# Second block's attention: value products of two pairs of heads' units in one go, six buffers for turned probabilities, the other heads' units placed by fours

## What is computed

```
heads = concat(o_a, o_b, o_c)
h = layer_norm(DEEPNORM_ALPHA * x + heads @ w_o, ln1_g, ln1_b)
ffn = (silu(h @ w_gate) * (h @ w_up)) @ w_down
return layer_norm(DEEPNORM_ALPHA * h + ffn, ln2_g, ln2_b)
```

## Time and profile before

| what | us |
|---|---|
| median of 3 runs | 1861.59 |
| the profiled execution | 1860.51 |
| its span in the trace | 1858.7 |
| TensorE busy in the span | 1830.9 |
| the attention loop, first layer of the second block | about 747 to 826 in the trace |
| the same, second layer | about 1360 to 1439 |

### The profile page before, as it was taken

One profiled execution on the slowest core, in us unless ns is written; L12 is line 12 of the kernel. 1 busy time (PEld: TensorE's weight loads), 2 busy tenths in 40 slices (PEclk: granted clock), 3 DMA queues, 4 the chain that ended last, 5 costly groups with the idle time before them and its releaser, 6 DMA issues.

```text
span 1858.7 us, 26490 instructions
## 1 busy us (share of the span) xinstructions
PE 1830.9 (99%) x10358; PEld 1532.0 (82%) x10358; DVE 771.7 (42%) x1679; ACT 802.7 (43%) x1571; POOL 790.6 (43%) x639
## 2 busy tenths in 40 slices
PE   8999999999999999999999999999999999999997
PEld 6888887888887888768888888888876898888886
DVE  4575575376473454876111110065377621111003
ACT  5222386472376565872323222127488233222213
POOL 2433372265553453334444444435322444444442
PEclk9999999999999999999999999999999999999999
DMA  9554412124402243103333333223310333333321
GB/s 331 195 151 152 131 46 69 57 91 141 138 24 71 71 139 95 58 25 91 91 110 95 91 94 133 87 87 108 118 47 19 94 102 100 91 91 113 114 91 45
DMA packets 195242, 185.60 MB, mean 100 GB/s; under 512 B 24150, under 2 KB 162564, under 8 KB 195120
## 3 DMA queue, kind: packets, MB, share of 16 engines
q1 hardware_dynamic: 180520, 172.51, 29.4%
q10 hardware_dynamic: 14600, 11.41, 2.2%
HBM read 179.11 MB, written 5.44 MB: 99 GB/s over the span
## 4 chain that ended last, share of the span: by engine, by line
PE 89%; ACT 4%; POOL 2%; DVE 2%; issue 1%; SPq 1%; DMA 1%; DVEq 0%; ACTq 0%; POOLq 0%
PE ps L1536 25%; PE ps L1538 25%; PE ps L1537 25%; PE ps L2079 3%; PE ps L2196 2%; PE ps L2175 2%; POOL w_lo L833 1%; PE ps L1598 1%; PE ps L1615 1%; PE ps L1631 1%; PE ps L2171 1%; ACT pt L1026 1%; ACT w_hi L968 1%; ACT sc L1016 1%; PE ps L1557 1%
## 5 line engine op out<-in xcount | busy, mean ns | idle before, releaser
L833 POOL TENSOR_TENSOR w_lo<-raw,w_hi 128x512 fp32r<-128x512 f32 (+1 forms) x505 | 671.0, 1360 | 828.3 <-ACT w_hi L968 828.1
L968 ACT ACTIVATE w_hi<-raw 128x1024 fp32r<-128x1024 f32 (+1 forms) x273 | 255.2, 980 | 262.6 <-PE ps L1538 190.9
L1536 PE MATMUL ps<-g_hi,w_lo 128*128 128x512 f32 (+1 forms) x928 | 348.4, 375 | 0.7 <-POOL w_lo L833 0.7
L1537 PE MATMUL ps<-g_lo,w_hi 128*128 128x512 f32 (+1 forms) x928 | 347.4, 374 | 0.0
L1538 PE MATMUL ps<-g_hi,w_hi 128*128 128x512 f32 (+1 forms) x928 | 347.4, 374 | 0.0
L1536 PEld LDWEIGHTS ps<-g_hi,w_lo 128*128 128x128 f32 x928 | 174.7, 188 | 33.0 <-POOL w_lo L833 1.1
L1537 PEld LDWEIGHTS ps<-g_lo,w_hi 128*128 128x128 f32 x928 | 174.7, 188 | 31.1
L1538 PEld LDWEIGHTS ps<-g_hi,w_hi 128*128 128x128 f32 x928 | 174.7, 188 | 31.0
L2940 DVE TENSOR_TENSOR tmp_f<-ps,tmp_f 128x512 f32<-128x512 f32 x44 | 30.4, 692 | 370.0 <-PE ps L1538 370.0
L1536 PE MATMUL ps<-h_hi,w_lo 128*128 128x512 f32 (+1 forms) x496 | 176.9, 357 | 0.1
L1537 PE MATMUL ps<-h_lo,w_hi 128*128 128x512 f32 (+1 forms) x496 | 174.6, 352 | 0.0
(11 more groups left out here) (305 smaller groups left out, 3229.6 us busy)
## 6 DMA issues: line engine op xcount, KB each, us to landing
raw<-in_w_in SPq DMA_DIRECT2D x33, 1024.0 KB, 5.1
raw<-in_w_mod SPq DMA_DIRECT2D x24, 1024.0 KB, 6.6
raw<-in_w_gate SPq DMA_DIRECT2D x44, 512.0 KB, 3.8
raw<-in_w_up SPq DMA_DIRECT2D x44, 512.0 KB, 4.9
raw<-in_w_down SPq DMA_DIRECT2D x22, 1024.0 KB, 4.8
raw<-in_w_out SPq DMA_DIRECT2D x8, 1024.0 KB, 5.0
strips<-bias_rows ACTq DMA_DIRECT2D x18, 256.0 KB, 4.1
raw<-in_w_o SPq DMA_DIRECT2D x4, 1024.0 KB, 4.9
```

Of the source, the lines that this page charges most:

```text
L833: pool.tensor_tensor(w_lo[:, i % SPLIT, a:e], raw_of(what)[:, a:e], w_hi[:, i % SPLIT, a:e].bitcast(F32), ALU.subtract).then_inc(s_tile_lo ...
L968: act.activation(w_hi[:, i % SPLIT, a:b], raw_of(what)[:, a:b], ACT.Copy).then_inc(s_tile_hi.sem, s_tile_hi.nth((what, n)))
L1536: pe.matmul(o, lhs[1], rhs[0], start=first, stop=False)
L1537: pe.matmul(o, lhs[0], rhs[1], start=False, stop=False)
```

## The change

`N_P` goes from 4 to 6. The two new buffers lie in parts of `qa` that nothing uses. `upto` becomes 4, 8, 12, 12, 16, 20, 24, 24, 28, 32, 36, 36, so the a and c units come in fours (two pairs), and after two of the 12 b pairs none come; 12 are left for the end. `DEFERRED` holds the ranks of 12 pairs a layer, the first pair of each four. Their value product is not made at its own place but directly ahead of that of the second pair, into columns 128 to 255 of the second pair's bank, and VectorE moves both out one after the other. The bank of a deferred rank is free as soon as ScalarE has copied the turned probabilities.

```diff
+        pt2 += [at(f"pt2_{4 + i}", [P, SEQ], names["qa"][0] + 4 * SEQ * (2 * i + 1)) for i in range(2)]
...
-                upto = 2 * ((n + 1) * 17 // len(pairs[EARLY // 2:]))
+                upto = 4 * -(-(n + 1) * 9 // len(pairs[EARLY // 2:]))
...
-        N_S, N_T, N_B, N_P = 3, 5, 5, 4
+        N_S, N_T, N_B, N_P = 3, 5, 5, 6
...
+        DEFERRED = set()
+        for r, i in enumerate(RANKS[:-2]):
+            if UNITS[i]["half"] == UNITS[RANKS[r + 2]]["half"] == 1 and r - 2 not in DEFERRED:
+                DEFERRED.add(r)
...
-                    if u["half"] == 0:
+                    if u["half"] == 0 or r in DEFERRED:
                         return
...
+                    for second, o in ((r - 2, P), (r, 0)) if r - 2 in DEFERRED else ((r, 0),):
+                        n = len(UNITS[RANKS[second]]["vs"])
+                        for j in range(n):
+                            for half in range(2):
+                                one = second - 1 + half
+                                m = pe.matmul(ps[HD * half:HD * half + HD, b, o:o + P], UNITS[RANKS[one]]["vs"][j],
+                                              pt2[one % N_P][:, P * j:P * j + P], start=j == 0, stop=j == n - 1)
+                        m.then_inc(s_mixed.sem, s_mixed.nth((y, second)))
...
-                        emptied[b] = s_pt.after((y, r)) if UNITS[i]["half"] == 0 else s_o_out.after((y, r))
+                        emptied[b] = s_pt.after((y, r)) if UNITS[i]["half"] == 0 or r in DEFERRED else s_o_out.after((y, r))
...
-                        V.tensor_copy(into, ps[:, b, 0:P]).then_inc(s_o_out.sem, s_o_out.nth((y, r)))
+                        for second, o in ((r - 2, P), (r, 0)) if r - 2 in DEFERRED else ((r, 0),):
+                            x = UNITS[RANKS[second]]
+                            into = ao_t[:, AO_T[CHUNK_OF[x["kind"], x["head"]]], P * x["i"]:P * x["i"] + P]
+                            V.tensor_copy(into, ps[:, b, o:o + P]).then_inc(s_o_out.sem, s_o_out.nth((y, second)))
```

More of the change, by code:

```diff
@@ L680, in _program @@
         LAST = len(RANKS) - 1
+        DEFERRED = set()
+        for r, i in enumerate(RANKS[:-2]):
+            if UNITS[i]["half"] == UNITS[RANKS[r + 2]]["half"] == 1 and r - 2 not in DEFERRED:
+                DEFERRED.add(r)
+        assert len(DEFERRED) == (A_HEADS + C_HEADS) // 2 * XT // 2 and not any(
+            r in DEFERRED and RANKS[r + 2] != RANKS[r] + 2 for r in range(len(RANKS)))
         MIXED_WITH = [r + 1 if UNITS[i]["half"] == 0 else r for r, i in enumerate(RANKS)]
@@ L2167, in mix @@
                         pe.wait_ge(s_proj.sem, s_proj.at((y, "vc", XT - 1)))
-                    n = len(u["vs"])
-                    for j in range(n):
-                        if u["half"] is None:
+                    if u["half"] is None:
+                        n = len(u["vs"])
+                        for j in range(n):
                             m = pe.matmul(ps[:, b, 0:HD], pt2[r % N_P][:, P * j:P * j + P], u["vs"][j], start=j == 0, stop=j == n - 1)
[L2172 to L2177, removed]
+                        m.then_inc(s_mixed.sem, s_mixed.nth((y, r)))
+                        return
+                    for second, o in ((r - 2, P), (r, 0)) if r - 2 in DEFERRED else ((r, 0),):
+                        n = len(UNITS[RANKS[second]]["vs"])
+                        for j in range(n):
+                            for half in range(2):
[3 more added lines that the diff above has]
+                        m.then_inc(s_mixed.sem, s_mixed.nth((y, second)))
                 for i in range(EARLY + 2, EARLY + N_S):
```

## The result

| | before | changed |
|---|---|---|
| median, us | 1861.37 (1860.95 to 1862.58, 4 runs) | 1880.70 (1879.21 to 1881.98, 4 runs) |
| profiled execution, us | 1860.51 | 1881.98 |
| its span in the trace | 1858.7 | 1880.2 |
| mean granted clock | 0.998 | 0.994 |
| loop of the first layer | 80.46 | 91.10 |

The changed kernel is slower: ratio 1.0102, interval 1.0087 to 1.0117, 19.3 us between the medians. The prediction was 1866.0, range 1856 to 1871.5, so the time lies outside it. A loop is counted here from the start of its first transposes to the start of the last record of its last value product; the row of that product has 4 records before and 12 in the changed kernel. The two loops together are 20.2 us longer, of 21.5 us in the spans: the change acted where it was made, and almost nowhere else.

What follows compares the result with a forecast made beforehand. TensorE was taken to set the pace. Per layer, savings of 3.25 and old waits of 1.6 gone against 7.4 of new waits gave +2.5, +5.1 in both: 1865.6, put at 1866.0 us, range 1856 to 1871.5.

Steps and rivals of the forecast that it cites:

- What bounds the kernel: Whole kernel and both attention loops: TensorE sets the pace, busy 77.3 of 78.9 us in the loop stretch, clock 1.00.
- What TensorE saves: Attention loops: 12 fewer visits and 21 fewer changes of arrangement a layer save 3.25 us a layer, 6.5 in both.
- Rival 4: Joint value products: two pairs in one go pay the surcharge again, only the new waits are left; 1872 us, chance 0.04.
- the drain of 0.053 us: TensorE's changes of tiling mode: about 128 cycles each at full clock, by which 42 fewer would save 2.2 us.
- units 29, 49, 55 and 61: TensorE's transposes waiting for VectorE's joinings: 3.0 us at units 27 to 29, then 2.0, 0.9 and 0.55 a layer.
- The lead sum: Unit 29: TensorE's 3.56 us between unit 28's scores and 29's transposes against VectorE's 5.1; at least 1.5 us of waiting.
- ScalarE's lateness: Steps 24 to 27: ScalarE has 5.1 us against TensorE's 3.95, so unit 27's exponential comes about 1.5 us late.
- No DMA and no GpSimd work moves: Whole change: DMA and GpSimd work stay where they were, counted at nothing.
- The parts at nothing: New buffers, copies out in twos, DMA, GpSimd and the rest of the kernel: no net cost, within 0.2 us for the rest.
- Units 67 to 72 and the end of the loop: Late in each loop: 0.6 us waiting for unit 73's score bank, and 0.35 at the end from copies and norm steps.
- gone from the old order: Old order's waits that vanish: 0.65 at the b3 pair, some 0.35 at 767.70, a few smaller; about 1.6 us a layer.
- Rival 1: Joinings: VectorE runs ahead, waits don't grow, only saved visits count; 1854.0, up to 1857.5 us, chance 0.18.

Runs made afterwards that it cites:

- the even order: Changed kernel with four other units behind each of the first nine b pairs, no two b pairs side by side, 11 pairs deferred: 1868.55 us, ratio 1.0042.

## Why the prediction was wrong

The direction was right, slower. The size was not: 4.6 us were forecast over the kernel before, 19.3 were measured.

**What bounds the kernel: right, but one quantity was taken as fixed.** TensorE sets the pace in the loops, and time was lost by making it wait and by what came behind the waits. The clock of 1.00 in the earlier trace rows was read as a property of the stretch. It held in a loop whose longest wait was some 0.8 us; behind waits of 1.3 to 2.3 us it was 0.50 for 17.0 us. Here is the step that failed: the sum prices a wait at its own length, at a clock of 1.00 throughout. What the clock costs behind a wait is absent from the sum and from every rival, and it is the largest single error: 7.6 us by the rows in those stretches (4.3 and 3.3), 9.5 by the comparison with filled waits. The span's mean clock says the same: 0.998 to 0.994 of 1880 us is 7.5.

The Trainium skill's page "TensorE: Matmul & The Clock Gate", Part 1, says that throttled is the default state of TensorE's clock and that activity releases it, and puts the cost of the ramp below 1% of a typical span. The trace agrees: falls behind waits, and 0.4 to 0.5% of this span. That is small on the page and twice what a measurement of this kernel can tell.

**What TensorE saves: right.** One surcharge for two pairs' products (1.25 and 1.24 us for five blocks), and work priced 3.38 us shorter a layer where 3.25 was said. Rival 4 is out. With the drain of 0.053 us, which the prediction worked out from the Trainium skill's page "TensorE: Matmul & The Clock Gate", the row would have taken 1.14 us, an estimate; measured is 1.25.

**The waits at the joinings: the places right, the two largest near in size, one cause wrong.** 6.45 us were put on units 29, 49, 55 and 61, 7.7 were found; unit 55 took half as much again as forecast and unit 61 twice as much. At units 27 to 29 the total came near by luck, 3.5 for 3.0. The lead sum gave 1.5 us and ScalarE's lateness another 1.5; in truth ScalarE costs 1.0 at unit 27 and the scores behind it and nothing at 29, and the joining itself is 0.92 longer than in the earlier trace rows. 1.5 + 0.92 = 2.4, of 2.31. The step that failed here is "No DMA and no GpSimd work moves". None moves in GpSimd's own order, but its subtraction starts when a chunk has been scaled, and the new order puts that just ahead of the joining of 28 and 29.

The Trainium skill's "GPSIMD Engine Reference", section Specifications, says that GpSimd and VectorE share SBUF interfaces, with contention where a VectorE instruction has two SBUF inputs. The trace agrees: the joining, with two, goes from 0.75 to 1.67 us, and the mask beside GpSimd's next operation, with one, stays at 0.55.

**The parts at nothing: mis-sized.** The copies in twos and the three score banks were "one step's delay of 0.2, hidden". Five waits for a bank of scores came to 1.8 us a layer. TensorE's next units hide the delay only where TensorE has them to do; ahead of a unit of three blocks behind a joining it does not. Units 67 to 72 and the end of the loop took 1.7 and 0.7, for 0.95 predicted.

**The sum.** Net waits +8.8 and +9.0 a layer for +5.8, though twice as much was gone from the old order as said (3.1 for 1.6). With the savings that alone is +10.7 us in both layers by the run with filled waits, so 1871.2 on the profiled execution's 1860.5, at the upper end of the range. The clock carried it beyond 1880. Of the 15.1 us by which the two loops missed the forecast's +5.1, 5.6 are waits and 9.5 the clock.

**The rivals.** All of them divided the same two terms, saving and waiting, and none had a place for a cost that grows out of waiting. Rival 1 is refuted: VectorE is not early at the joinings. The range ended at 1871.5 because "what a late unit passes on" was given 2.5 us; the clock behind it took three to four times that.

**What stays open.** Whether a wait is followed by a fall of the clock is not settled by its length: 2.09 us was followed by one, 1.80 in the same place of the other layer was not, and of the changed kernel's variants each had its falls at other places. With the deferral alone a fall from 802.7 stood behind waits of 0.94 and 0.99, and with GpSimd held back one began before unit 29's wait was over, behind 0.79, 0.39 and 0.65. By their mean clocks the executions of one kernel differ in it too. That long waits bring the falls is shown by two runs: with the waits filled there was none in the loops, and a long wait added to the kernel before brought one. When a given wait does so can't be told from these runs. Nor is the rest of the 0.9 us at the end of the loop taken apart, and what the even order costs without the deferral was not run.

## What to carry to other kernels

Where TensorE sets the pace, price an idle stretch of one to two microseconds at up to twice its length, since its clock may be halved behind it (the same added wait of 1.6 us cost 3.1 with a fall and 1.6 without), and count such places in the new order before counting what is saved. Before work of the pacing engine is put off or put together, ask what it covered at its old place: a product of 0.6 us moved behind a dependent step is 0.6 us less for the other engine to be ready in. And when an order moves, list what every queue starts as a consequence, since an operation with two SBUF inputs may lie beside GpSimd's.

## What the hardware showed unexpectedly

- TensorE's granted clock fell from 1.00 to 0.50 (2.4 to 1.2 GHz) inside an attention loop in which it was busy for over 90% of the time. It did so behind waits, for 3.4 or 6.8 us. Before the first of these stretches TensorE had been busy for 5.1 of 6.8 us:

```profile
767.80:774.60 6.80, 5.10 (x26) 3.03 (x24) 5.21 (x17) 6.13 (x18) 1.63 (x2) 1.00 0.00 0
```

- Useless products in the place of four waits a layer made the kernel 5.9 us faster, though they ran 1.8 us a layer over.
- A VectorE operation with two SBUF inputs of 512 columns took 1.67 us beside a GpSimd operation with two inputs, and 0.75 alone. The one that began second was the one that got longer. GpSimd's that was running took 1.26, as elsewhere; its next, begun during the joining, took 1.72. In the six runs in which a four-block joining began beside a running GpSimd subtraction it ended 0.55 us behind that one's end, all twelve times, though it took from 1.38 to 1.68 in all.
